# Token rows turned before the layer norm is known and corrected in the bank, with constant products ahead of two waits of TensorE

## The reference, cut to what matters

```python
def residual_block(h, so, mo, w_o, g1, b1, g2, b2, w_r1, b_r1, w_r2, b_r2, w_gate, w_up, w_down):
    mix = jnp.concatenate([so.reshape(B, T, QS), mo.reshape(B, T, QM).astype(so.dtype)], -1) @ w_o
    h = layer_norm(DN_ALPHA * h + mix, g1, b1)
    return layer_norm(DN_ALPHA * h + hier_moe(h, w_r1, b_r1, w_r2, b_r2, w_gate, w_up, w_down), g2, b2)

def hier_moe(h, w_r1, b_r1, w_r2, b_r2, w_gate, w_up, w_down):
    g_prob = jax.nn.softmax((xt @ w_r1).astype(F32) + b_r1, axis=-1)
    p_grp, grp = lax.top_k(g_prob, 1)                       # 1 of 4 groups
    e_all = jnp.einsum('nd,gde->nge', xt, w_r2).astype(F32) + b_r2
    e_logit = jnp.take_along_axis(e_all, grp[:, :, None], axis=1)[:, 0]
    p_e, e_idx = lax.top_k(jax.nn.softmax(e_logit, axis=-1), 2)
    hid = jax.nn.silu(einsum(xt, w_gate)) * einsum(xt, w_up)
    y = einsum(hid * gate, w_down)
```

## Time and profile before

| | |
|---|---|
| median of 3 runs | 2555.03 us (2531.79 to 2558.09) |
| the profiled execution | 2555.98 us, of which its span is 2554.1 us |
| mean granted TensorE clock | 0.945 |
| TensorE busy (PE) | 2334.0 us, 91% of the span |
| VectorE (DVE), ScalarE (ACT) busy | 657.3 us, 496.6 us |
| HBM | 640.16 MB read, 5.96 MB written, 253 GB/s over the span |

### The profile page before, as it was taken

One profiled execution on the slowest core, in us unless ns is written; L12 is line 12 of the kernel. 1 busy time (PEld: TensorE's weight loads), 2 busy tenths in 40 slices (PEclk: granted clock), 3 DMA queues, 4 the chain that ended last, 5 costly groups with the idle time before them and its releaser, 6 DMA issues.

```text
span 2554.1 us, 31866 instructions
## 1 busy us (share of the span) xinstructions
PE 2334.0 (91%) x12357; PEld 1435.8 (56%) x12357; DVE 657.3 (26%) x1219; ACT 496.6 (19%) x1101; POOL 4.2 (0%) x10
## 2 busy tenths in 40 slices
PE   6999999989598999898999998999995999999997
PEld 4678785678433434343578885545783344434445
DVE  0259911502622121212300000122026112121213
ACT  1220116500310101010310016623003110100014
POOL 0000000000000000000000000000000000000000
PEclk9999999989679999999999999988996799999998
DMA  8523457764029898989645456988330498989890
GB/s 272 179 100 132 163 160 242 248 243 161 33 114 428 346 428 365 429 352 428 235 128 149 147 167 236 363 312 289 141 129 34 208 427 347 429 364 428 352 402 34
DMA packets 210104, 647.65 MB, mean 254 GB/s; under 512 B 56826, under 2 KB 90251, under 8 KB 184123
## 3 DMA queue, kind: packets, MB, share of 16 engines
q1 hardware_dynamic: 174618, 636.28, 64.6%
q10 hardware_dynamic: 35376, 9.91, 1.7%
HBM read 640.16 MB, written 5.96 MB: 253 GB/s over the span
## 4 chain that ended last, share of the span: by engine, by line
PE 76%; DMA 12%; DVE 4%; ACT 4%; ACTq 2%; issue 1%; SPq 0%; DVEq 0%
PE bank L596 17%; PE bank L1132 11%; PE bank L1117 9%; PE bank L1018 8%; PE bank L1162 7%; DMA ring<-in_w_down 6%; DMA ring<-in_w_up 5%; PE bank L1176 5%; PE bank L774 4%; PE bank L783 2%; PE bank L914 2%; ACT arena L1247 2%; ACTq L383 1%; PE bank L895 1%; ACT X L1461 1%
## 5 line engine op out<-in xcount | busy, mean ns | idle before, releaser
L1132 PE MATMUL bank<-ring,AT 128*64 128x512 f32 x2048 | 456.2, 604 | 31.9 <-DMA ring<-in_w_up 30.1
L1247 ACT ACTIVATE arena<-bank 128x512 f32<-128x512 f32 (+4 forms) x543 | 269.5, 544 | 935.8 <-PE bank L596 414.9
L596 PE MATMUL bank<-X,ring 128*128 128x264 f32 x1664 | 373.9, 388 | 1.2 <-ACT arena L1247 1.2
L596 PEld LDWEIGHTS bank<-X,ring 128*128 128x128 f32 x1664 | 317.9, 191 | 56.2 <-ACT arena L1247 1.4
L1132 PEld LDWEIGHTS bank<-ring,AT 128*64 128x64 f32 x2048 | 148.3, 139 | 331.5 <-issue 295.5
L1162 PE MATMUL bank<-ring,arena 128*64 128x512 f32 x1024 | 225.0, 594 | 31.2 <-DMA ring<-in_w_down 18.5
L1018 PE MATMUL bank<-AT,ring 128*128 128x264 f32 x1024 | 238.9, 397 | 8.1 <-DVEq L1799 8.1
L1117 PE MATMUL bank<-arena 128*128 128x256 bf16 (+1 forms) x1440 | 220.9, 301 | 5.6 <-DVE arena L1888 5.6
L1018 PEld LDWEIGHTS bank<-AT,ring 128*128 128x128 f32 x1024 | 200.4, 196 | 44.5 <-issue 8.9
L2034 DVE TENSOR_TENSOR X<-bank,X 128x264 f32<-128x264 f32 x256 | 110.6, 432 | 386.4 <-PE bank L1176 383.3
L1117 PEld LDWEIGHTS bank<-arena 128*128 128x128 bf16 (+1 forms) x1440 | 122.2, 103 | 108.4 <-issue 84.1
(11 more groups left out here) (284 smaller groups left out, 1456.7 us busy)
## 6 DMA issues: line engine op xcount, KB each, us to landing
ring<-in_w_gate SPq DMA_DIRECT2D x64, 2048.0 KB, 16.2
ring<-in_w_up SPq DMA_DIRECT2D x64, 2048.0 KB, 12.8
ring<-in_w_down SPq DMA_DIRECT2D x64, 2048.0 KB, 16.6
ring<-in_w_o SPq DMA_DIRECT2D x16, 2048.0 KB, 9.5
ring<-in_cache_b_k SPq DMA_DIRECT2D x128, 256.0 KB, 4.2
ring<-in_cache_b_v SPq DMA_DIRECT2D x128, 256.0 KB, 4.6
ring<-in_w_in_a SPq DMA_DIRECT2D x14, 2048.0 KB, 9.1
ring<-in_w_in_b SPq DMA_DIRECT2D x12, 2048.0 KB, 8.3
```

What stands on the lines that cost most here:

```text
L596: mm = pe.matmul(B[4 * (g % 2) + f][:, 0:n_tok], u[:, c * 512 + f * P:c * 512 + (f + 1) * P], src[8 * half + c][:, 0:n_tok], start=(half = ...
L1132: mm = pe.matmul(B[bank][64 * s:64 * s + 64, :], M.xsT[:, at:at + 64], ring[slots[s][0]][:, c * FE:(c + 1) * FE], start=(half == 0 and c = ...
L1247: return act.activation(out, in_, ACT.Copy, scale=scale)
```

## The change

The order of the normalisation is turned round. With x the centred sum, g the gain, b the shift, m what is left of the mean and s the deviation, the normalised value is (g·x − g·m + b·s) / s. So:

- ACT multiplies X by the gain in place (`gains`), before the statistics are known. The router logits are taken from this product, and the scaled copy of the router weights (`M.wrg`) goes.
- TensorE turns g·x into token rows at once (`raw_rows`, a product with the identity where `transpose` stood), and adds the correction to the bank by a product of two rows of weights, −m and s (`M.fix`), with two rows g and b of 512 features (`M.gain`), one such product an item (`fix_rows`; two for each sample item). `M.gain` comes by two small DMAs a layer, behind a new wait in the SP queue.
- The division by s moves into ACT's and DVE's split of the rows, as a scale per token (`M.c1[8]`). TensorE brings s into token order with four tiny products, and the router's bias with another.
- X itself is normalised, scaled and shifted only after the selection is made: DVE `normalise` stands behind `extra_entries`, and ACT adds the shift behind the first gather's copies.
- Four banks (`ROW_BANKS`) instead of three hold rows, and the second selection matrix of `pick(0)` (`sg12`) is written behind the last low part.
- Ahead of TensorE's waits for `chosen` and for `low_made` stand four products each of constants with constants, 128 x 128 by 512 float32, into bank 3, which nobody reads (`idle_products`).

```diff
+                sp.wait_ge(S("mixed"), 12 * layer + 1)
+                for k, w in enumerate(("ln1_g", "ln1_b")):
+                    sp.dma_start(M.gain[k:P:32, :], i[w][layer].rearrange("(q f) -> q f", q=4)).then_inc(S("gain_rows"), 16)
...
-                    mm = pe.matmul(B[2][:, 0:T], M.wrg[:, 20 * c:20 * c + P], Xc[c], start=(c == 0), stop=(c == KC - 1))
+                    pe.wait_ge(S("ln_scaled"), KC * layer + c + 1)
+                    mm = pe.matmul(B[2][:, 0:T], wr[:, 20 * c:20 * c + P], Xc[c], start=(c == 0), stop=(c == KC - 1))
...
                                 pe.matmul(B[1][:, 0:T], cst("mean"), M.sqs, start=True, stop=False)
-                                pe.wait_ge(S("wr_scaled"), 2 * (layer + 1))
-                                raw_logits(layer, range(12))
+                                raw_logits(layer, range(8))
...
+                raw_logits(layer, range(8, 12))
...
-                    pe.matmul(B[3][:, 0:T], cst("mean"), Xc[c], start=(c == 12), stop=(c == KC - 1))
-                    mm = raw_logits(layer, [c])
+                    pe.matmul(B[3][:, 0:T], cst("mean"), Xc[c], start=(c == 12), stop=(c == KC - 1))\
+                      .then_inc(S("ln_shift"), 1)
                 squares(k_ln, range(12, KC))
+                raw_logits(layer, range(12, KC)).then_inc(S("raw_logits"), 1)
+
+            def idle_products(n):
+
+                for _ in range(n):
+                    pe.matmul(B[3][:, :], cst("ones"), consts[:, 0:512], start=True, stop=True)
...
-            def token_rows(layer, items):
-
-                base = N_ITEMS * layer
...
-                    for c in range(4):
-                        if t < 2:
-                            mm = pe.transpose(B[4 + n % 3][:, c * P:(c + 1) * P],
-                                              Xc[4 * q + c][:, t * P:(t + 1) * P], ident)
...
-                    mm.then_inc(S("token_rows"), 1)
+            def raw_rows(layer, n):
+
+                q, t, _ = row_item(n)
+                bank = B[ROW_BANKS[n % 4]]
+                pe.wait_ge(S("ln_scaled"), KC * layer + (4 * q + 4 if t < 2 else KC))
+                if n >= 4:
+                    pe.wait_ge(S("rest_made"), N_ITEMS * layer + n - 3)
+                for c in range(4):
+                    if t < 2:
+                        pe.matmul(bank[:, c * P:(c + 1) * P], Xc[4 * q + c][:, t * P:(t + 1) * P], ident,
+                                  start=(c == 0), stop=False)
+                    else:
+                        for g in range(2):
+                            pe.matmul(bank[64 * g:64 * g + NB, c * P:(c + 1) * P],
+                                      Xc[8 * g + 4 * (n - 8) + c][:, SEQ:T], ident, start=(c == 0), stop=False)
+
+            def fix_rows(layer, n):
+
+                q, t, _ = row_item(n)
+                bank = B[ROW_BANKS[n % 4]]
+                if t < 2:
+                    mm = pe.matmul(bank[:, :], M.fix[32 * q:32 * q + 2, t * P:(t + 1) * P], M.gain[32 * q:32 * q + 2, :],
+                                   start=False, stop=True)
+                else:
+                    for g in range(2):
+                        rows = slice(32 * (2 * g + n - 8), 32 * (2 * g + n - 8) + 2)
+                        mm = pe.matmul(bank[64 * g:64 * g + NB, :], M.fix[rows, SEQ:T], M.gain[rows, :],
+                                       start=False, stop=True)
+                mm.then_inc(S("token_rows"), 1)
 
             def experts(layer):
                 sm = lambda name: S(f"{name}_l{layer}")
 
+                for n in range(4):
+                    raw_rows(layer, n)
                 pe.wait_ge(S("logits_copied"), layer + 1)
+                one = ident[0:20, 0:20]
...
-                    pe.transpose(B[7][:, 64 + 20 * t:84 + 20 * t], M.lgT[:, t * P:(t + 1) * P], ident[0:20, 0:20])
+                    pe.transpose(B[7][:, 64 + 20 * t:84 + 20 * t], M.lgT[:, t * P:(t + 1) * P], one)
...
+                pe.wait_ge(S("ln_std"), 2 * layer + 1)
+                for t in range(2):
+                    pe.matmul(B[7][:, 124 + t:125 + t], M.rstd[0:1, t * P:(t + 1) * P], ident[0:1, 0:1], start=True, stop=True)
+                for g in range(2):
+                    mm = pe.matmul(B[7][64 * g:64 * g + NB, 126:127], M.rstd[0:1, SEQ:T], ident[0:1, 0:1],
                                    start=True, stop=True)
-                mm.then_inc(S("logit_rows"), 1)
-                token_rows(layer, range(4))
-
+                mm.then_inc(S("router_rows"), 1)
+                pe.wait_ge(S("fix_ready"), layer + 1)
+                pe.wait_ge(S("gain_rows"), 32 * (layer + 1))
...
+                for n in range(4):
+                    fix_rows(layer, n)
+                for n in range(4, 6):
+                    raw_rows(layer, n)
+                    fix_rows(layer, n)
+
+                idle_products(4)
                 pe.wait_ge(S("chosen"), layer + 1)
...
                 mm.then_inc(S("ranks"), 1)
-                token_rows(layer, range(4, N_ITEMS))
+                for n in range(6, N_ITEMS):
+                    raw_rows(layer, n)
+                    fix_rows(layer, n)
+                idle_products(4)
...
+            def gains(layer, cs):
+                for c in cs:
+                    if c >= 12:
+                        act.wait_ge(S("ln_shift"), 4 * layer + c - 11)
+                    act.activation(Xc[c], Xc[c], ACT.Copy, scale=lnp[:, 16 * layer + c:16 * layer + c + 1])\
+                       .then_inc(S("ln_scaled"), 1)
+
+            def norm_sums(layer):
+                k = 2 * layer
+                load_table(ACT.Sqrt)
+                squares(k, range(12))
+                gains(layer, range(12))
+                squares(k, range(12, KC))
+                gains(layer, range(12, KC))
                 act.wait_ge(S("ln_var"), k + 1)
-                act.activation(M.rstd, M.rstd, ACT.Sqrt).then_inc(S("ln_std"), 1)
...
+            def row_high(layer, n):
+
+                _, t, out = row_item(n)
+                act.wait_ge(S("token_rows"), N_ITEMS * layer + n + 1)
+                src = B[ROW_BANKS[n % 4]][:, :].rearrange("r (p j) -> r j p", j=8)
+                act.activation(out[0], src, ACT.Copy, scale=M.c1[8][:, t:t + 1]).then_inc(S("high_made"), 1)
...
-                affine(2 * layer, range(0, 4))
+                act.wait_ge(S("row_scale"), layer + 1)
                 router_exp(0)
-                affine(2 * layer, range(4, 8))
-                row_parts(layer, range(2))
+                row_high(layer, 0)
+                row_high(layer, 1)
                 router_exp(1)
-                affine(2 * layer, range(8, 12))
-                row_parts(layer, range(2, 4))
-                affine(2 * layer, range(12, 16))
-                row_parts(layer, range(4, N_ITEMS + 1))
+                for n in range(2, N_ITEMS + 2):
+                    if n < N_ITEMS:
+                        row_high(layer, n)
+                    row_mid(layer, n - 2)
                 def gather_copies(done):
                     for q in range(8):
                         act.wait_ge(sm("gathered"), done * 8 + (q + 1))
...
-                for k in range(4):
-                    x = X[:, k * 4 * T:(k + 1) * 4 * T]
-                    copy(x, x, ALPHA).then_inc(S("scaled"), 1)
+                for c in range(KC):
+                    act.wait_ge(S("ln_normed"), 32 * layer + c + 1)
+                    act.activation(Xc[c], Xc[c], ACT.Identity, bias=M.ab[:, c:c + 1]).then_inc(S("ln_out"), 1)
...
+                dve.wait_ge(S("ln_shift"), 4 * (layer + 1))
+                link(dve.tensor_copy(M.sh, B[3][:, 0:T]))
+                link(dve.tensor_tensor(M.sqs, M.sh, M.sh, ALU.mult))
+                link(dve.tensor_scalar(M.fix, M.sh, cst("row_mean"), None, ALU.mult))
                 dve.wait_ge(S("ln_square_used"), 16 * k_ln + KC)
-                link(dve.tensor_copy(M.sh, B[3][:, 0:T]))
-                link(dve.tensor_tensor(M.rstd, M.sh, M.sh, ALU.mult))
-                link(dve.scalar_tensor_tensor(M.rstd, M.rstd, -1.0, B[1][:, 0:T], ALU.mult, ALU.add))
-                dve.tensor_scalar(M.rstd, M.rstd, EPS, None, ALU.add).then_inc(S("ln_var"), 1)
-                shift(layer, 0)
+                dve.scalar_tensor_tensor(M.rstd, M.sqs, -1.0, B[1][:, 0:T], ALU.mult, ALU.add).then_inc(S("ln_var"), 1)
+                dve.wait_ge(S("raw_logits"), layer + 1)
+                dve.scalar_tensor_tensor(M.lgT, M.sh[0:20, :], M.lb[:, 0:1], B[2][0:20, 0:T], ALU.mult, ALU.add)\
+                   .then_inc(S("logits_copied"), 1)
                 dve.wait_ge(S("ln_std"), k_ln + 1)
+                dve.scalar_tensor_tensor(M.fix, M.rstd, cst("row_std"), M.fix, ALU.mult, ALU.add).then_inc(S("fix_ready"), 1)
+
+            def normalise(layer):
+
                 link(dve.reciprocal(M.rstd, M.rstd))
-
-                link(dve.scalar_tensor_tensor(M.lgT, M.sh[0:20, :], M.lb[:, 0:1], B[2][0:20, 0:T], ALU.mult, ALU.add))
```

(31 more changed lines are left out.)

108 lines of the change are left out of this document (49 added, 59 removed).

## The result

The change makes the kernel 1.5% faster: 2512.70 us median (2504.79 to 2517.61, 4 runs) against 2556.56 (2531.79 to 2559.34, 4 runs), a ratio of 0.9847 with a 95% interval of 0.9814 to 0.9880. That is 43.9 us, where 28.7 were forecast. The profiled execution took 2504.79 us, the fastest of the four, with a span of 2503.2 us, 50.9 less than before, and a mean granted clock of 0.967 against 0.945.

The account below looks back on a forecast made before the run. TensorE, busy 91% of the span, was taken as the bound. Per layer 14.9 (gather) + 1.2 (gate products) − 1.8 (later start) = 14.3 us, 28.7 in two: 2556.0 − 28.7 = 2527.3; the range reached to 2550 and took in 2496 and 2511.

Parts of the forecast that it names:

- The main step: First gather of each layer: runs at 2.4 GHz, 19.1 us each, 14.9 us off.
- the sum: Router stage up to the gather: its terms added up, the gather starts 1.8 us later than before.
- The fourth rival: Before or in the gather: the clock comes back and is lost again, 34 us stay; 2560 us, chance 0.08.
- The covers: Router stage and gather: last low part ready under the constants, moved normalisation free behind the gather, TensorE's waits near zero.
- the corrections of items 0 to 3: Router stage, after the raw rows: two-row products on TensorE take 6.3 us, ending at 669.4.
- items 6 to 9: Router stage, after the ranks: the clock falls again; items 6 and 7 end at 693.0, 8 and 9 take 7.6 us.
- The first four constants: Ahead of the choice: 5.6 us, ending 11 us after the choice is made, costing what the ladder gained.
- the ladder: Router stage before the change: TensorE's waits for logits (6.08 us), shifted tiles (2.73), choice (3.91) and last low parts (2.81).
- The second: Whole router stage: the clock holds throughout, gather starts 13.7 us earlier; 2496 us, chance 0.15.
- The third: Router stage: the clock holds for about half of it, first or second; 2511 us, chance 0.10.
- the first rival: The forecast itself: the clock falls twice in the stage, the gather is fast; 2512 to 2540 us, chance 0.62.
- fifth: Stage and gather: TensorE at 1.2 GHz throughout, constants included, 13 us a layer later; 2582 us, chance 0.05.

Follow-up runs that it names:

- e4: The kernel before, rows and order untouched, with four constant products added ahead of the wait for the last low parts; median 31.3 us below the kernel before.
- e8: The changed kernel with all corrections reading their two rows from rows 0 and 1; its stage was 9.0 us a layer longer than in the unaltered changed kernel.
- e6: The changed kernel with each set of four constants replaced by 26 transposes of 128x128 float32; 2515.93 us.
- e7: The changed kernel with two constants between the corrections of items 0 to 3 and item 4, none ahead of the choice, the last four kept; 2507.63 us.
- the control: The changed kernel itself, unaltered, timed again in a second set of four executions; 2516.68 us.
- e2: The changed kernel without the four constants ahead of the wait for the choice, the last four kept; 2512.65 us.
- e1: The changed kernel without its eight constant products a layer; 2528.81 to 2548.19 us, median 10.3 us below the kernel before.
- e5: The changed kernel with all eight constants of a layer given 2 rows of weights and data in place of 128; 2556.59 us.
- e3: The changed kernel without the four constants ahead of the wait for the last parts, the first four kept; 2524.60 to 2539.78 us.
- e9: The changed kernel with no constants ahead of the choice and two in place of four ahead of the gather; 2509.83 us.

## Why the prediction was right, and where its sizes were off

- **The main step** held to a tenth of a microsecond: both gathers went from 34.0 to 19.1 us (14.9 and 15.0), and the gate products from 29.19 to 27.69 (1.5 for 1.2). e4, which makes no other change, gives most of the gain by this step alone. One reading of the profile before was wrong without harm to the sum: the clock does not fall in the 2.8 us wait, but 0.4 us into the gather. The fourth rival has it right.
- **The covers** held: `chosen` is not waited for, `low_made` 0 and 0.45 us, DVE waits 6.85 us for the ranks, the late normalisation is hidden. Of the sizes of the sum, the raw logits ended at 657.15 (657.4 forecast), the rows of items 0 to 3 at 660.7 (661.6), items 4 and 5 took 8.0 us (8.2), the first constants 5.4 (5.6), the ranks 2.3 (2.6).
- **Mis-sized: the corrections of items 0 to 3.** 6.3 us were forecast, one behind the other. They took 2.0, with a wait of 1.65 us behind them, so 2.6 us less (e8 shows the cause: two groups of rows side by side). The wait was not seen because in the sum TensorE came too late to meet it.
- **Mis-sized: items 6 to 9.** The step was that the clock falls again after the ranks. It did not. Items 6 and 7 took 4.3 us for 7.2, and items 8 and 9 took 5.5 for 7.6 in layer 0, and 3.9 in layer 1, where the last constants fell to 3.7 as well. For the four items that is 5.0 and 6.6 us less. The fall after the ranks is real in e6, e7 and e8, so what failed was to give a single place to something that shifts by microseconds.
- **The sum** of these and some small terms: the gather starts 7.9 and 11.2 us earlier in the profiled execution (7.9 and 7.8 in the control) instead of 1.8 later. So the sign that it would start within 4 us of 704 failed, and with it the one of a low clock from the ranks to the second constants. Twice some 9.6 is 19 us over the forecast for a usual run. 15.2 of it arrived in the median of the first batch and 5.5 in that of the control, and the rest of the span and the kernel before move by as much as the difference. Both errors point the same way, and the range was wide enough for them.
- **The first four constants** were said to cost what the ladder gained. They shorten the stage by 2.7 us a layer (the control against e2), by warming what stands behind them. The time does not show it.
- **The rivals.** The second, a clock that holds by real products, is excluded by e1. The third, a clock up in about half of the stage, is near what happened, at 2511: the clock was low for 20.5 us of the stage in layer 0 and for 10.2 in layer 1. By its time the run stands at the edge of the first rival (2512 to 2540) and on the third. What the forecast had right is the gather; of the stage it had the first fall and the first return of the clock, and not what came behind them. The fourth and fifth fell with the gather rows. e1 shows the price that they named, a cold gather of 34.3 us; in the profile of e5 it was 26.4.

## What to carry to other kernels

Look for stretches in which TensorE is full and yet slow: the price of a short wait stood in the 34 us behind it, and four products whose result nobody reads, put into that wait, bought 31 us without touching anything else, where the whole change brought 34 to 44. Fill waits in front of long runs with products of 128 rows of weights, only as many as the wait is long, and price small products at either clock, since the same program meets a different one from layer to layer. Place products of few rows in different groups of 32 rows: four corrections over two groups took the time of two.

## What the runs showed of the hardware that was not expected

- A gather of 144 bfloat16 products straight behind constants of 128 rows or transposes, or behind such constants and a wait of up to 0.46 us, runs at 2.4 GHz (19.10 to 19.35 us). Behind a wait of 2.8 to 4.1 us, or behind constants of 2 rows, it runs at 1.2 GHz for 16 us (26.39) or nearly throughout (33.98 to 34.31), though it has no gaps. Both lengths were met in one launch (e3). What decides between them is open.
- The clock at its first product does not decide it. Before the change it was 1.00 and fell 0.4 us later; in e9 it was 0.50 and rose 0.5 us later.
- Eight constants of 2 rows, 7 us of full work at each place, left the clock at 0.50. Those of 128 rows brought it back before the set was over, and so did the first transposes; behind the second set it rose as the gather began.
- Four corrections of 512 columns in two groups of rows take 2.0 us, four in one group 5.5 us with the clock falling after the first 1.7.
- In the same kernel the clock fell at +21.5 us after the first mean product in layer 0 and at +23.9 in layer 1, and the second stage was 3.4 us shorter.
